# The first states come in four transfers of two row blocks each, the border column comes with the parameters, and one Exp is run early

## What is computed

```python
def modulate_norm(h, g, shift, scale):
    return rms_norm(h, g) * (1.0 + scale) + shift

for i in range(DEPTH):                                   # DEPTH = 2
    mod = silu(c) @ mod_w[i] + mod_b[i]                  # six parts: shift, scale, gate, twice
    u = modulate_norm(h, norm_mix_pre[i], s1, sc1)
    if i % N_MIXERS == 0:
        b_gate, c_gate, xp = jnp.split(u @ w_in, 3, axis=-1)
        y = (b_gate * dwconv3(c_gate * xp, conv_k)) @ w_out
    else:
        y = block_attention(...) @ attn_w_o[j]
    h = gated_residual(h, y, norm_mix_post[i], g1)
    u = modulate_norm(h, norm_ffn_pre[i], s2, sc2)
    h = gated_residual(h, conv_ffn(u, ffn_w_up[i], ffn_conv[i], ffn_w_down[i]), norm_ffn_post[i], g2)
```

## Time and profile before

| | us |
|---|---|
| median of 3 runs | 2530.21 |
| runs | 2528.87 to 2577.18 |
| profiled execution, slowest core (core 0) | 2531.3 |
| spans of the eight cores in it | 2514.1 to 2531.3 |
| PE busy in it | 2382.3 (94%) |
| DVE, ACT, POOL busy | 1571.8, 1347.7, 1196.1 |

### The profile page before, as it was taken

How to read it: one execution, slowest core, us unless ns; L and a number is a source line. 1 busy time by engine, 2 the same in 40 slices (tenths; PEclk the granted TensorE clock), 3 DMA queues, 4 the chain that set the end, 5 groups by cost and what they waited for, 6 DMA issues and landing times.

```text
span 2531.3 us, 37635 instructions; the slowest of 8 cores (2514.1 to 2531.3 us)
## 1 busy us (share of the span) xinstructions
PE 2382.3 (94%) x12993; PEld 1089.1 (43%) x12993; DVE 1571.8 (62%) x1747; ACT 1347.7 (53%) x1849; POOL 1196.1 (47%) x1106
## 2 busy tenths in 40 slices
PE   1898999999999999999889999999999999999998
PEld 0343444444444444444444333333444444444446
DVE  0556586666366727772795788397497637746752
ACT  1333443544347525443787888799654435534433
POOL 1147462854466648455464234320354455546434
PEclk9999999999999999999999999999999999999999
DMA  9456846365376644644425400100355465439621
GB/s 183 97 105 126 174 83 121 56 106 96 69 154 131 133 81 85 117 83 89 76 39 104 145 11 13 30 1 1 67 87 89 71 131 123 106 69 180 112 50 68
DMA packets 75226, 231.93 MB, mean 92 GB/s; under 512 B 9248, under 2 KB 14880, under 8 KB 75040
## 3 DMA queue, kind: packets, MB, share of 16 engines
q0 software_dynamic: 48512, 170.55, 40.0%
q1 hardware_dynamic: 26528, 58.98, 7.2%
HBM read 370.65 MB, written 29.36 MB: 158 GB/s over the span
## 4 chain that ended last, share of the span: by engine, by line
PE 78%; DMA 6%; DVE 4%; issue 4%; ACT 4%; POOL 2%; another core or an unknown queue 1%; SPq 0%; DVEq 0%; ACTq 0%; POOLq 0%
PE ps L668 38%; PE ps L601 22%; PE ps L1022 6%; PE ps L1032 5%; PE ps L872 3%; DMA h<-x_in 2%; DMA wr<-win 2%; DVE ra L700 1%; POOL rs L487 1%; PE ps L1049 1%; PE ps L493 1%; ACT yb L101 1%; PE ps L932 1%; DMA h<-h_mem 1%
## 5 line engine op out<-in xcount | busy, mean ns | idle before, releaser
L668 PE MATMUL ps<-u,wr 128*128 128x512 bf16 x5328 | 1187.8, 382 | 25.2 <-DMA wr<-win 15.9
L668 PEld LDWEIGHTS ps<-u,wr 128*128 128x128 bf16 x5328 | 513.8, 98 | 640.1 <-issue 48.2
L700 DVE SCALAR_TENSOR_TENSOR ev<-ps,par,ev 128x1023 f32<-128x1023 f32 (+1 forms) x336 | 428.5, 1281 | 165.8 <-ACT ev L101 134.2
L601 PE MATMUL ps<-ra,wr 128*128 128x512 bf16 (+1 forms) x2338 | 508.9, 378 | 11.8 <-ACT sqb L101 3.7
L101 ACT ACTIVATE wr<-ps 128x1024 bf16<-128x1024 f32 (+1 forms) x352 | 329.3, 984 | 46.9 <-PE ps L1022 45.9
L601 PEld LDWEIGHTS ps<-ra,wr 128*128 128x128 bf16 x2338 | 227.5, 98 | 287.0 <-issue 21.0
L101 ACT ACTIVATE ev<-ps,par 128x1024 f32<-128x1024 f32 x168 | 186.6, 1111 | 225.0 <-PE ps L668 221.6
L700 DVE SCALAR_TENSOR_TENSOR ra<-ps,par,ra 128x1023 f32<-128x1023 f32 (+1 forms) x192 | 243.3, 1278 | 37.3 <-ACT ra L101 25.4
L786 POOL TENSOR_TENSOR ra<-ev 128x1023 bf16<-128x1023 f32 (+1 forms) x84 | 199.2, 2371 | 141.9 <-ACT ev L101 68.5
L487 POOL TENSOR_TENSOR rs<-rs,sqb 128x512 f32<-128x512 f32 (+1 forms) x125 | 183.3, 1475 | 123.9 <-ACT sqb L101 122.5
L1032 PE MATMUL ps<-wr,ra 128*128 128x512 bf16 x640 | 193.3, 381 | 4.9 <-DVE ra L1059 2.6
(11 more groups left out here) (182 smaller groups left out, 2702.0 us busy)
## 6 DMA issues: line engine op xcount, KB each, us to landing
wr<-wup POOLq DMA_DIRECT2D x132, 512.0 KB, 6.3
wr<-wdn POOLq DMA_DIRECT2D x41, 704.0 KB, 6.5
wr<-modw POOLq DMA_DIRECT2D x40, 512.0 KB, 7.0
wr<-win POOLq DMA_DIRECT2D x24, 768.0 KB, 9.9
h_mem<-h SPq DMA_DIRECT2D x24, 512.0 KB, 7.4
h<-h_mem SPq DMA_DIRECT2D x24, 512.0 KB, 5.5
h_out<-h SPq DMA_DIRECT2D x40, 256.0 KB, 6.2
h<-x_in SPq DMA_DIRECT2D x16, 512.0 KB, 10.8
```

Of the source, the lines that this page charges most:

```text
L601: ins = e.matmul(bank(b, n), w3[:, k, :], rhs(k), start=(k == 0), stop=(k == nk - 1))
L668: ins = e.matmul(bank(b + ct), lhs_fn(kc), ub.ap[:, kc, ct * 512:ct * 512 + 512], start=(kc == 0), stop=(kc == KC - 1))
L700: P.dve(lambda e, ro=ro, zi=zi, w=w: e.scalar_tensor_tensor(out=ro, in0=zi, scalar=w, in1=ro, op0=ALU.mult, op1=ALU.add), 1024, rd + wr, w ...
```

## The change

`x_in` is laid out by unit: three blocks of 128 partitions, in each of which a unit's eight row blocks lie one after the other, so that two row blocks are one run of 8 KB per partition. S0 is loaded by four transfers of 128 x 2048 float32, issued right behind `params` with nothing between them. S1 and P are still loaded by eight transfers of 128 x 1024. The border column is put into `params` as eight more columns (476 instead of 468), and the transfer into `hcol` is gone from the opening; `norm_halo` reads the parameters there. One Exp on a column of `params`, written into the scratch `hc2` and read by nothing, is recorded with priority -99.

```diff
@@ -31,7 +31,8 @@
 P_CVEC = P_KG + 1
 P_EPS = P_CVEC + 16
 P_SPLIT = P_EPS + 1
-P_N = P_SPLIT + 1
+P_XB = P_SPLIT + 1
+P_N = P_XB + 8
 
 
 class Op:
@@ -262,7 +263,7 @@
     def dout(name, shape):
         return nc.dram_tensor(name, list(shape), F32, kind="ExternalOutput").ap()
 
-    x_in = din("x_in", [128, KC, TT])
+    x_in = din("x_in", [3, 128, KC * 1024])
     params = din("params", [128, P_N])
     modw = din("modw", [2, 24, 128, KC * 256])
     win = din("win", [8, 128, KC * 384])
@@ -450,7 +451,8 @@
             for ct in cts:
                 for kc in range(KC):
                     a, b = (0, 1024) if ct is None else (ct * 512, ct * 512 + 512)
-                    P.dma("sp", hap(U, kc, a, b), src[:, kc, U.ui * 1024 + a:U.ui * 1024 + b], 128 * (b - a) * 4,
+                    frm = x_in[U.ui, :, kc * 1024 + a:kc * 1024 + b] if src is x_in else src[:, kc, U.ui * 1024 + a:U.ui * 1024 + b]
+                    P.dma("sp", hap(U, kc, a, b), frm, 128 * (b - a) * 4,
                           reads=([("hm", U.ui, kc)] if src is h_mem else []) + list(cur["k"] if after is None else after),
                           writes=hk(U, kc, 0) + hk(U, kc, 1) if ct is None else hk(U, kc, ct))
                     yield
@@ -542,16 +544,17 @@
                     out=o, in0=t, scalar1=mv[:, bpart * 8 + kc, U.v:U.v + 1]), 350,
                     tk + modk(l, bpart, kc), ok, sh=True)
 
-        def norm_halo(l, ai, bpart):
+        def norm_halo(l, ai, bpart, hc=None):
             mv, cf = mvs[l], cfs[l]
-            P.act(8, "sb", [("hcol",)], [("hsq",)], hsq_t, hcol_t, AF.Square)
+            hc, hck = hc or (hcol_t, [("hcol",)])
+            P.act(8, "sb", hck, [("hsq",)], hsq_t, hc, AF.Square)
             P.pe(lambda e: e.matmul(bank(7, 8), ones_d, hsq_t, start=True, stop=True), 0.05, [("hsq",), ("ones",)], pk(7))
             ss, th = hc2_t[:, 8:9], hc2_t[:, 0:8]
             P.dve(lambda e: e.tensor_reduce(out=ss, in_=bank(7, 8), axis=mybir.AxisListType.X, op=ALU.add), 60, pk(7), [("hss",)])
             P.act(1, "sb", [("hss",), ("par",)], [("hss",)], ss, ss, AF.Ln, bias=eps_ap)
             P.act(1, "sb", [("hss",)], [("hss",)], ss, ss, AF.Exp, scale=-0.5)
-            P.dve(lambda e: e.tensor_tensor(out=th, in0=hcol_t, in1=cf[:, ai, :, 0], op=ALU.mult), 60,
-                  [("hcol",)] + cfk(l, ai), [("th",)])
+            P.dve(lambda e: e.tensor_tensor(out=th, in0=hc, in1=cf[:, ai, :, 0], op=ALU.mult), 60,
+                  hck + cfk(l, ai), [("th",)])
             P.dve(lambda e: e.scalar_tensor_tensor(out=uh_t, in0=th, scalar=ss, in1=mv[:, bpart * 8:bpart * 8 + 8, 0],
                                                    op0=ALU.mult, op1=ALU.add), 60,
                   [("th",), ("hss",)] + modk(l, bpart), [("uh",)])
@@ -1168,16 +1171,20 @@
                 for p in ps_:
                     for part in (1, 0):
                         P.dma("pool", mods[part, p][0], modw[0, part * 4 + p], 128 * 4096, writes=mods[part, p][1])
-            at(-100.0, lambda: run(load_h(U, x_in, 0, cts=(0,), after=())))
+            U.slot = 0
+
+            def rows(p):
+                P.dma("sp", h_t[0][:, p * 2048:(p + 1) * 2048], x_in[U.ui, :, p * 2048:(p + 1) * 2048], 128 * 8192,
+                      writes=[k for kc in (2 * p, 2 * p + 1) for ct in range(2) for k in hk(U, kc, ct)])
+            at(-100.0, lambda: [rows(p) for p in pairs])
             at(-99.0, lambda: fetch(0, 1))
-            at(-98.0, lambda: run(load_h(U, x_in, 0, cts=(1,), after=mods[0, 0][1])))
             box = []
             at(-97.0, lambda: box.append(load_w(win[0], KC * 384)))
             w, wk = box[0]
             w3 = w.rearrange("p (k n) -> p k n", n=384)
             at(-96.0, lambda: fetch(2, 3))
-            P.dma("sp", hcol_t, x_in[:, :, 1024], 4096, writes=[("hcol",)], allow_slow_non_contiguous=True)
             P.dma("pool", sel_t, sel, 131072, writes=[("sel",)])
+            at(-99.0, lambda: P.act(1, "sb", [("par",)], [("hss",)], hc2_t[:, 8:9], par[:, P_EPS:P_EPS + 1], AF.Exp))
             xh = []
             for ct in range(2):
                 norm_stats(U, ct, 7, sq="act", groups=range(KC))
@@ -1212,7 +1219,7 @@
                                                start=(kc == 0), stop=(kc == KC - 1))
                             return ins
                         P.pe(f, MM * 2, wk + [q for kc in (2 * p, 2 * p + 1) for q in ub.keys(kc, ct * 512, ct * 512 + 512)], pk(b + ct))
-            norm_halo(0, 0, 0)
+            norm_halo(0, 0, 0, (par[:, P_XB:P_XB + 8], [("par",)]))
             cur["k"] = ub.keys(7, 512, 513)
             return w, wk, sets
 
@@ -1337,7 +1344,8 @@
         xs = inp["x_sample"][b]
         xp = inp["x_prompt"][4 * b:4 * b + 4].reshape(TP, D)
         xa = np.concatenate([xs, xp], axis=0)
-        m["x_in"] = f(xa.reshape(TT, KC, 128).transpose(2, 1, 0))
+        p[:, P_XB:P_XB + 8] = xs[1024].reshape(KC, 128).T
+        m["x_in"] = f(xa.reshape(3, 1024, KC, 128).transpose(0, 3, 2, 1).reshape(3, 128, KC * 1024))
         m["ckT"] = f(inp["cache_k"][b, 0].transpose(2, 1, 0)[pm])
         m["cvl"] = f(inp["cache_v"][b, 0].reshape(4, 128, 256).transpose(1, 0, 2))
         in_maps.append(m)
```

## The result

The changed kernel takes **0.989 of the time before (0.987 to 0.991)**. Its two undisturbed executions took 2506.09 and 2507.53 us, beside 2528.87 to 2531.82 before. That is 23.5 us less by these times and 28 by the ratio (22 to 33 by its interval), where 26 were predicted. The interval leaves out 1, but the change is smaller than the 2% that a measurement of this kernel has to show to count as faster.

A forecast was written before the change was run, and what follows sets the result against it. The prediction took the opening, up to the first L668 at 82.83 us, as serial time held by `hcol` and late states. Savings of 21.3 + 5 = 26 us off 2531.3 gave 2505, as a median 2504; range 2494 to 2516.

The forecast's parts named there:

- The landing order: Opening's transfers: states in by 29 to 31 us, sixth `modw` at 43.2, last near 50, next `win` near 55.
- the first rival: State transfers: 8 KB rows take two turns, states end near 44 us, gain 17 + 5, 2508 us; chance 0.13.
- Ct 0's Ln "ready near 34": ACT in the opening: the Ln of ct 0 ready near 34 us, covered by the fifth `modw` near 40.
- The cover of the fifth `modw`: Opening: the fifth `modw`, near 40 us, hides ct 0's Ln and its table load, 34 against 40.
- The step behind the sixth `modw`: Opening: from its landing at 43.2 us, matmuls until 45.5, then Ln and Exp until the first `yb` multiply at 47.6.
- DVE's work behind it: Opening, after DVE's wait: multiplies, `u` and small operations, 0.5 us for waits, until 58.4; first L671 at 61.5.
- The stage: Behind the opening: 5 of 12.6 us saved, first `win` stall (3.9) gone, second about 1 us shorter; bounds 0 and 12.6.
- The sum: Whole kernel: 21.3 us from the opening plus 5 from the stage, 26 us off.
- The edits at nothing: Opening: larger params and an additional and a repeated table load cost nothing; bare, each load is 1.3 us.
- stalls vanishing whole: Rival on the stage: both `win` stalls go entirely, 21 + 12.6 us saved, 2496 us; chance 0.17.
- the stage did not take back: Rival on the stage: late opening loads slow its transfers, stalls grow by up to 8 us, 2517 us; chance 0.07.
- weights starve: Rival on the opening: long rows starve the weight queue, opening ends at 90 us, 2537 us; chance 0.01.

The follow-up runs named there:

- e9: The changed kernel with the S0 states in eight transfers with 4 KB rows instead of four with 8 KB; one execution 2518.43 us beside 2531.97 before.
- e7: The changed kernel with the planner given the landing times of the opening's transfers from the trace, so only the order changes; ratio to before 0.9881.
- e5: The changed kernel with the planner told S1's states are four times as large, so POOL issues block 4's `win` ahead of two sums; ratio to before 0.9877.
- e3: The changed kernel without the early Exp, that one line taken out; ratio to before 0.9886.
- e2: The changed kernel with the border column fetched in 4-byte pieces behind the four state transfers, and without the early Exp; ratio to before 0.997.
- e1: The kernel before with only the border column moved into `params`, states still in 16 transfers of 2 KB rows; ratio to before 0.9982.

## Why the prediction was right

**The landing order: right.** The pair of rows was priced at 0.38 + 0.43 = 0.81 us, and 0.40 + 0.41 was measured. States land at 10.1, 16.4, 22.7 and 29.0 us (the last at 28 to 31 on the eight cores), predicted by 29 to 31. The sixth `modw` lands at 42.3 (43.2), the last at 49.6 (near 50), the second `win` at 53.7 (55). The two turns of the first rival are false here; `e9` shows what they would have cost, 44 us for the last state, just the rival's figure.

**Ct 0's Ln "ready near 34": wrong, and without effect.** It came at 38.19. What the step left out is the ring of squares and ACT's order: ahead of the last two squares of ct 0 stand two of ct 1, and those waited for places that the PE gives back only behind the fourth `modw` (33.23 in the ACT rows). In `e7`, whose order has it otherwise, the Ln came at 33.20. The cover of the fifth `modw` held by 0.8 us: `rs` is ready at 39.6, `ev` starts at 40.44 (40.3 predicted). It had been written down as a gap of six.

**The step behind the sixth `modw`: 1.2 us too long.** The first `yb` multiply came at 46.44, not 47.6, mainly because the block was in 0.9 us earlier. That DVE's wait there is 2.00 us, as predicted, is luck: the seven operations ahead of it were put at 5.3 us and took 4.0 (40.44 to 44.44), which is also what the prediction's own prices give (5 x 0.62 + 2 x 0.45); with these and `yb` at 47.6 it should have said 3.3.

**DVE's work behind it: 1.3 us too short.** From `yb` to the first L671 15.2 us passed and not 13.9. The prices of `yb`, `ev` and `u` held. The 0.5 us "for waits" was the term mis-sized: DVE waits 1.18 and 1.11 us for `modw` matmuls that stand behind L1218 on the PE. The two errors cancel, so 61.65 against 61.5 looks better than the working was. The saving is 21.2 us against the 82.83 from which the prediction started (21.3 predicted), 21.5 against the same core before (83.19), and 22.4 in the mean of the cores, which were at 83.3 before and at 60.9 after.

**The stage: mechanism right, size 5 against 3.1.** The first stall went on all cores, and the reason given bears up: `wr<-modw` goes out at the stage's start, and in `e7`, where it goes out late again, the stall is back. But it was priced at 3.9 us by core 0, of which 1.7 were slow matmuls. In the mean of the cores the stall is 1.5 us, and on seven of them 3.61 us follow it and no slow ones. The second stall fell from 5.6 to 3.8 us in the mean (1 us predicted), but not on the slowest core, where it is 7.72. That its `win` need not be waited for when it stands earlier on POOL's queue is shown by `e5`; that this `win` also takes 8 us on some cores and 12 or 13 on others was not in the prediction.

**The sum: right, with some luck.** Opening and stage were put at 21.3 and 5, together 26.3, and gave 22.4 and 3.1 in the mean of the cores, together 25.5. One was too low and the other too high, and the errors of 1.1 and 1.9 us partly cancel.

**The edits at nothing: right** (`e3`). **The rivals:** stalls vanishing whole would have been `e5`'s order, not this one; the stage did not take back, nor did weights starve. Behind the stage nothing moved.

**What the prediction did not see** is that another order of the opening was worth 6 us more in it (`e7`): the fifth and sixth `modw` decide only because the planner, which reckons by bytes, put their matmuls ahead of work that was ready.

## What to carry to other kernels

Where two queues share the DMA engines, count turns and not bytes: longer rows on one queue shift the schedule of the other (the sixth `modw` went from 37.1 us to 42.3 here), and 1024 pieces of four bytes held SP's queue in `e2` for 28 us, as long as 4 MB of states in long rows ahead of them. When two things hold the same moment, test them together, since each alone shows almost nothing (3.9 and 2.2 of 22.4 us). And after a change to transfers look at what each engine's queue is made to wait behind: a planner with wrong landing times leaves some of the gain lying, and a weight transfer that stands behind a sum of late data has no slack left for the times when it is slow itself.

## What the runs showed of the hardware

**Rows of 8 KB take one turn.** The four transfers of the states were 512 packets of 8192 bytes, and from 10 to 28 us the two queues moved 398 and 405 packets. The Trainium skill, DMA: Bandwidth & Descriptors (SWDGE vs HWDGE vs iDMA), puts a packet at 4096 B preferably; for these transfers from SP the traces show no such limit. The same page's rule of alternation (Queues, rings and completion order) held in all three row lengths: 840 to 841 packets with 2 KB, 950 to 969 with 4 KB (`e9`), 398 to 405 with 8 KB.

**A long stall costs slow matmuls besides.** On core 6 the PE waits 7.72 us; in the 5 us behind, its granted clock is 0.57, near the lower of its two levels (1.2 of 2.4 GHz), and 16 matmuls, of which the trace has 15, take 5.51 us:

```profile
95.00:103.00 8.00, 0.28 (x12) 0.33 (x11) 3.80 (x3) 2.36 (x4) 1.67 (x2) 0.63 1.00 198
103.00:108.00 5.00, 5.00 (x14) 1.89 (x14) 0.00 (x0) 1.26 (x2) 2.07 (x3) 0.57 1.00 161
```

On core 1 the same wait is 1.15 us, and 16 matmuls behind it take 3.61 at full clock:

```profile
94.94 3.61 PE L671 MATMUL ps<-u,wr 128*128 128x512 bf16 x16 [1.15 <-DMA wr<-win]
```

So the second stall costs 7.72 + 1.9 us on one core and 1.15 on another. Between the two groups of cores the stages differ by less, 86.6 and 82.1 us in the mean, since the four with the short wait stand 1.5 to 2.4 us for S1's squares later on and the others don't. Waits between these two go either way: in `e1` 3.25 us are followed by 3.61 for 16 matmuls on core 3 and by 5.30 on core 6.

**A table load is 1.28 us and nothing more.** The Trainium skill, ScalarE: Activation LUTs (What ACT_TABLE_LOAD costs), gives 1283 ns and a DRAIN of some 1380 ns beside it. The load agrees. No drain is seen: the Exp starts at 5.26 us behind a load of 3.97 to 5.25, the Ln at 38.19 behind one of 36.89 to 38.17.
